# Decoder layer on one core: the FFN step in two token halves, low value weights last, and another end stage

## The chip, the cores and the metric

The kernel runs on 1 core of one Trainium2 chip. The metric is the device time of one execution in microseconds (us), lower is better. Engines: PE (TensorE matmul; PEld its weight loads), DVE (VectorE), ACT (ScalarE), POOL (GpSimd), SP (SyncE, which issues the DMAs here). They run side by side and are ordered by semaphores alone.

## The reference

One decoder layer on 512 tokens of width 1024, then a last RMSNorm, all in float32:

```
h  = RMSNorm(x) * (1+scale1) + shift1;  proj = h @ w_in
merged = sigmoid(gA) * (hgrn2(proj) @ W_a) + sigmoid(gB) * (attention(proj) @ W_b)
x  = x + (1+gate1) * (merged @ w_out)                        # w_out 1024x1024
h2 = RMSNorm(x) * (1+scale2) + shift2
u_gate, u_val = split(h2 @ w_up)                             # w_up 1024x5632
x  = x + (1+gate2) * ((gelu(causal_conv3(u_gate)) * u_val) @ w_down)
out = RMSNorm(x)
```

## The kernel before, in words

Every float32 product is made of three passes: an operand `a` is split in a high part (ACT copies it to fp32r) and a low part (`a - high`, a subtraction), and PE adds high*high, low*high and high*low in one PSUM bank. Weights come in units of 1 MB through two raw buffers, slots 0 and 1. For each unit SP issues the load (L465) once the slot's last unit is split, ACT makes the high part (L659, one instruction), POOL the low part (L590, four). Units 38 to 41 are `w_out` (the out-projection), 42 to 63 are `w_up`, in turn a gate unit and a value unit, and 64 to 74 are `w_down`.

**Out-projection.** Each of the four units makes four tiles (tokens t = 0..3, 128 tokens by 256 columns, 8 k steps of 3 matmuls). DVE multiplies a tile by the row of (1+gate1) into an SBUF buffer `sgb` (L1620) and adds it to the residual stream `x1` (L1622). ACT squares the new columns and sums them (L870). After the last unit's columns DVE adds up the four sums of a tile (L1628), POOL makes `rstd` of it in two instructions (L551, L552), and ACT or DVE scales the tile to `xn_ffn` (L878: tiles 0, 1 and half of 3; L1647: tile 2 and half of 3).

**Hand-over to the FFN step.** PE transposes the 4 x 8 blocks of `xn_ffn`, tile by tile, into 8 banks (L937). Per k block (128 features by 512 tokens) DVE makes `h_tmp2` with scale and shift (L1339), ACT makes `h_hi` (L891), and the low part `h_lo` is made on DVE (even k and k = 1, L1301) or POOL (odd k from 3, L583). On POOL these stand behind the low part of unit 43, the first value unit. Then a loop of 11 turns runs, each a gate unit and a value unit of 48 matmuls of 512 columns; the gate unit runs k outermost over two banks and in its first turn waits for `h_lo` of each k. ACT and DVE do the convolution, GELU and product with the value (L898 to L1675).

**End stage.** The down product fills the 8 banks `y(t, half)` (512 columns each). In the last unit they become ready one by one. For each, DVE multiplies by the row of (1+gate2) into `gelu` (L1685) and adds it to `x1` (L1686); ACT squares (L921); POOL multiplies tiles 0 and 1 by the final gain into `xg` (L645), and for every tile adds the two sums (L648) and makes `rstd` (L551, L552). ACT scales `xg` (L914) for tiles 0, 1 and 3; DVE makes `xg` of tile 3 (L1688) and the whole of tile 2 (L1691). SP sends each piece out (L526).

## Time and profile before

| | |
|---|---|
| median of 3 runs | 1010.56 us (1008.28 to 1012.77) |
| the profiled execution | 1011.39 us, its span 1009.7 us |
| PE busy | 954.7 us, 95% of the span, 4911 matmuls |
| DVE / ACT / POOL busy | 466.9 / 367.9 / 463.4 us |
| DMA | 111.33 MB, queue q1 33.3% |
| PE granted clock, mean | 0.982 |
| the output's DMAs, issue to landing | 2.6 us for 512 KB, 2.1 us for 256 KB (medians) |

Start times in rows are us from the span's start. A row of the timeline has the start, the duration, the engine, the line and the operation; in brackets stands how long the engine sat idle before it and what released it. A matmul's duration is longer than the distance to the next one, since they are pipelined. PEclk 1.00 is full speed.

### The profile page before, as it was taken

The page shows a single profiled execution, that of the slowest core. Times are in us where ns is not written, and L with a number is a line of the kernel's source. Part 1 is how long each engine was busy: PE and PEld are TensorE (multiplying, and loading weights), DVE is VectorE, ACT ScalarE, POOL GpSimd, SP SyncE. Part 2 cuts the span into 40 slices and gives each one's busy share as a digit, 9 for nine tenths or more (in the row PEclk, how much of TensorE's full clock was granted, in tenths as well). Part 3 has the DMA queues.
Part 4 walks back from the last instruction along what each step waited for, and adds up shares of the span by engine and source line. Part 5 has one row for each costly group of instructions (what it writes and reads, how often), then busy time and mean ns, then how long its engine had stood idle before and what let it go on. Part 6 is the DMA issues. An engine that isn't in the chain of part 4 may idle for free.

```text
span 1009.7 us, 12653 instructions
## 1 busy us (share of the span) xinstructions
PE 954.7 (95%) x4911; PEld 812.8 (80%) x4911; DVE 466.9 (46%) x720; ACT 367.9 (36%) x499; POOL 463.4 (46%) x382
## 2 busy tenths in 40 slices
PE   2699999999999989899999999899999999999995
PEld 2578989998888878788778899688888888888884
DVE  5855366665337858886642554622222322200006
ACT  6443332424234141444222334544435544412113
POOL 3669542534123243534455455553543453453544
PEclk9989999999999989999999999999999999999998
DMA  9722222121151756362222533123223223223212
GB/s 322 223 83 84 84 84 84 43 84 43 43 167 43 242 175 217 117 209 84 83 84 84 188 101 109 42 83 122 86 83 125 83 83 109 100 87 122 84 42 83
DMA packets 94817, 111.33 MB, mean 110 GB/s; under 512 B 1930, under 2 KB 88118, under 8 KB 94774
## 3 DMA queue, kind: packets, MB, share of 16 engines
q1 hardware_dynamic: 94774, 110.72, 33.3%
q8 instruction: 31, 0.51, 0.2%
q14 instruction: 12, 0.10, 0.0%
HBM read 108.62 MB, written 2.10 MB: 110 GB/s over the span
## 4 chain that ended last, share of the span: by engine, by line
PE 43%; issue 31%; POOL 18%; DVE 5%; ACT 1%; DMA 1%; SPq 0%; POOLq 0%; ACTq 0%; DVEq 0%
PE bank L934 43%; POOL w_lo L590 17%; DVE x L1686 1%; DVE part L1284 1%; DMA x_in<-in_x_dram 1%; DVE h_lo L1301 1%; DVE gelu L1685 0%; DVE part L1295 0%; DVE ada L1284 0%; DVE part L1286 0%; DVE ada L1286 0%; ACT w_hi L659 0%; DVE part L1291 0%; POOL rstd L551 0%; ACT xn_in L703 0%
## 5 line engine op out<-in xcount | busy, mean ns | idle before, releaser
L590 POOL TENSOR_TENSOR w_lo<-w_raw,w_hi 128x512 fp32r<-128x512 f32 x292 | 395.8, 1386 | 494.1 <-ACT w_hi L659 494.1
L934 PE MATMUL bank<-h_hi,w_hi 128*128 128x512 f32 x832 | 332.8, 400 | 9.1 <-POOL w_lo L590 6.0
L934 PE MATMUL bank<-h_hi,w_lo 128*128 128x512 f32 x832 | 329.1, 396 | 0.0
L934 PE MATMUL bank<-h_lo,w_hi 128*128 128x512 f32 x832 | 328.7, 395 | 0.0
L659 ACT ACTIVATE w_hi<-w_raw 128x2048 fp32r<-128x2048 f32 x73 | 139.4, 1909 | 238.1 <-PE bank L934 180.8
L934 PEld LDWEIGHTS bank<-h_hi,w_hi 128*128 128x128 f32 x832 | 159.8, 192 | 44.4 <-POOL w_lo L590 6.2
L934 PEld LDWEIGHTS bank<-h_hi,w_lo 128*128 128x128 f32 x832 | 159.0, 191 | 33.9
L934 PEld LDWEIGHTS bank<-h_lo,w_hi 128*128 128x128 f32 x832 | 159.7, 192 | 32.9
L934 PE MATMUL bank<-w_lo,act_hi 128*128 128x512 f32 x176 | 68.5, 389 | 0.0
L934 PE MATMUL bank<-w_hi,act_lo 128*128 128x512 f32 x176 | 68.5, 389 | 0.0
L934 PE MATMUL bank<-w_hi,act_hi 128*128 128x512 f32 x176 | 68.5, 389 | 0.0
L1660 DVE SCALAR_TENSOR_TENSOR conv<-bank,convc,conv 128x511 f32<-128x511 f32 x22 | 16.4, 745 | 107.8 <-ACT conv L898 107.8
L1685 DVE TENSOR_TENSOR gelu<-bank,g_row 128x512 f32<-128x512 f32 x8 | 5.5, 682 | 107.9 <-PE bank L934 107.9
L1284 DVE SCALAR_TENSOR_TENSOR part<-ada,csilu,part 128x256 f32<-128x256 f32 x64 | 43.8, 685 | 0.0
L1670 DVE TENSOR_TENSOR gelu<-gelu,bank 128x512 f32<-128x512 f32 x22 | 15.1, 687 | 58.3 <-PE bank L934 45.2
L898 ACT ACT_TABLE_LOAD x11 | 14.1, 1283 | 73.8 <-PE bank L934 73.8
L934 PEld LDWEIGHTS bank<-w_hi,act_hi 128*128 128x128 f32 x176 | 33.0, 188 | 6.9
L934 PEld LDWEIGHTS bank<-w_hi,act_lo 128*128 128x128 f32 x176 | 33.0, 188 | 6.9
L934 PEld LDWEIGHTS bank<-w_lo,act_hi 128*128 128x128 f32 x176 | 33.0, 188 | 6.7
L1284 DVE SCALAR_TENSOR_TENSOR ada<-ada,csilu 128x256 f32<-128x256 f32 x56 | 37.4, 669 | 0.0
L934 PE MATMUL bank<-w_hi,m_hi 128*128 128x256 f32 x128 | 36.3, 284 | 0.3 <-POOL w_lo L590 0.3
L934 PE MATMUL bank<-w_hi,h_hi 128*128 128x256 f32 x128 | 36.5, 285 | 0.0
(247 smaller groups left out, 1329.2 us busy)
## 6 DMA issues: line engine op xcount, KB each, us to landing
w_raw<-in_w_in_dram SPq DMA_DIRECT2D x32, 1024.0 KB, 5.2
ada<-in_w_ada_dram SPq DMA_DIRECT2D x24, 1024.0 KB, 7.2
w_raw<-in_w_up_dram SPq DMA_DIRECT2D x22, 1024.0 KB, 5.1
w_raw<-in_w_down_dram SPq DMA_DIRECT2D x11, 1024.0 KB, 4.8
w_raw<-in_w_out_dram SPq DMA_DIRECT2D x4, 1024.0 KB, 6.5
x_in<-in_x_dram SPq DMA_DIRECT2D x4, 512.0 KB, 7.1
w_raw<-in_w_in_dram SPq DMA_DIRECT2D x8, 256.0 KB, 8.5
w_raw<-in_w_branch_a_dram SPq DMA_DIRECT2D x2, 1024.0 KB, 4.9
```

Of the source, the lines that this page charges most:

```text
L590: ins = pool.tensor_tensor(wlo[slot][:, cols], raw[slot][:, cols], whi[slot][:, cols].bitcast(F32), ALU.subtract)
L659: act.activation(whi[bufs][:, :], raw[bufs][:, :], ACT.Copy).then_inc(hi_done, 1)
L898: act.activation(conv[:, t, :], bank[t][:, :], ACT.Identity, scale=CW[:, bass.ds(2 * i + (2 * FT + t), 1)], bias=CW[:, bass.ds(2 * i + (3 ...
L934: return pe.matmul(o, lhsT, rhs, start=start, stop=stop, **kw)
L1284: ins = stt(dst, unit[:, k, :], sc, dst, ALU.mult, ALU.add)
L1301: tt(h_lo[:, k, :], h_part(which, k), h_hi[:, k, :].bitcast(F32), ALU.subtract).then_inc(h_lo_done[k % 2], 1)
L1660: stt(tt_, bank[t][:, 0:S - 1], CW[:, bass.ds(2 * i + (FT + t), 1)], tt_, ALU.mult, ALU.add).then_inc(tap_done, 1)
L1670: tt(gelu[:, t, :], gelu[:, t, :], bank[bk][:, :], ALU.mult).then_inc(free[bk], 1)
L1685: link(tt(gelu[:, half, :], b[:, :], g2_row[:, cols], ALU.mult))
L1686: tt(x1[:, t, cols], x1[:, t, cols], gelu[:, half, :], ALU.add).then_inc(x2_done, 1)
```

## The change

1. Out-projection: DVE multiplies inside the PSUM bank and adds from there to `x1`; `sgb` is not used.
2. Last out-projection unit (41): the order of DVE is written out in `last_tiles`; the mean of the first three column sums is taken beforehand (`mean3`), so that POOL needs one instruction (`root2`) per tile. In PE's last tile, tokens 384 to 511, the transposes of tokens 0 to 255 stand between k = 3 and k = 4.
3. The gate unit's first turn is taken out of the loop and runs in two token halves of 256 columns, each 8 k steps of 6 matmuls. The transposes of the second half stand behind k = 5 of the first half. `h_tmp2`, `h_hi` and `h_lo` are made per half, two k blocks to a bank. Transposes use banks 4 to 7; the gates use banks 0 and 2, which the last out-projection tile (bank 1) doesn't use; the values use 1 and 3.
4. First value unit (43): the 32 matmuls with its high weights come first, then the 16 with the low ones; on ACT and POOL its split comes later than before. In all later value units k is outermost and both banks end together.
5. End stage: multiply inside the bank as in 1; POOL weighs tiles 0, 1, half of 2 and half of 3, DVE finishes the other halves in one instruction each; the last two roots are one POOL instruction each; the last four output pieces are 256 KB each.

The diff, cut to its core, in the order planner of the banks, POOL, ACT, PE, DVE:

```diff
-    for k in range(KT):
-        use(("xT", 1, k), "gates" if k < 3 else "small")
+    for half in range(2):
+        for j in range(KT // 2):
+            use(("xT2", half, j), "turn")
     base = list(uses)
-    for i, name in enumerate(("gate0", "gate1", "val0", "val1")):
+    last = table["g", U_UP - 1, 3][0]
+    for name, i in zip(("gate0", "gate1", "val0", "val1"), [b for b in range(3) if b != last] + [last, 3]):
...
+            def low_h2(half, k):
+                pool.wait_ge(h2_hi_done, half * KT + k + 1)
+                pool.tensor_tensor(h_lo[:, k, HALF[half]], h2_part(half, k), h_hi[:, k, HALF[half]].bitcast(F32),
+                                   ALU.subtract).then_inc(h2_lo_done[half][1], 1)
...
+            def root2(t):
+                pool.wait_ge(ssq_done, t + 1)
+                pool.tensor_tensor(rstd[:, TT + t:TT + t + 1], ssq[:, TT + t:TT + t + 1], mhalf[:, 0:1],
+                                   ALU.pow).then_inc(rstd_done, 1)
...
-            for t in range(TT):
-                pool.wait_ge(ssq_done, t + 1)
-                inverse_root(TT + t, 1)
-            low_part(U_UP + 1, 1)
-            pool.wait_ge(h_lo_done[1], KT // 2 + 1)
-            for k in range(3, KT, 2):
-                low_h(1, k)
+            for t in range(TT - 1):
+                root2(t)
+            low_h2(0, 1)
+            root2(TT - 1)
+            for k in range(3, KT, 2):
+                low_h2(0, k)
+            for k in range(1, KT, 2):
+                low_h2(1, k)
+            low_part(U_UP + 1, 1)
...
+            def final_weight(t, cols):
+                pool.wait_ge(x2_done, 2 * t + (2 if cols.stop == D else 1))
+                pool.tensor_tensor(xg[:, t, cols], x1[:, t, cols], gf_row[:, cols], ALU.mult).then_inc(xg_done, 1)
+            def last_root(t):
+                col = 2 * TT + t
+                pool.wait_ge(mean_last, t - (TT - 2) + 1)
+                pool.tensor_tensor(rstd[:, col:col + 1], ssq[:, col:col + 1], mhalf[:, 0:1], ALU.pow).then_inc(rstd_done, 1)
...
+            for t in range(TT - 2):
+                final_weight(t, slice(0, D))
...
                 inverse_root(col, 1)
+            final_weight(TT - 2, slice(512, D))
+            last_root(TT - 2)
+            final_weight(TT - 1, slice(0, 512))
+            last_root(TT - 1)
...
+                        if u == U_UP - 1 and t == 2:
+                            xn_again(0, slice(0, D))
+                        if u == U_UP - 1 and t == TT - 1:
+                            for k in range(2):
+                                high_h2(0, k)
...
+            def high_h2(half, k):
+                j = k // 2
+                b, n = BANKS["xT2", half, j]
+                if k % 2:
+                    evacuated(act, ("xT2", half, k // 2))
+                else:
+                    act.wait_ge(h2_tmp_done, half * KT // 2 + k // 2 + 1)
+                act.activation(h_hi[:, k, HALF[half]], h2_part(half, k), ACT.Copy).then_inc(h2_hi_done, 1)
...
+            for k in range(2, 6):
+                high_h2(0, k)
             xn_again(TT - 1, slice(512, D))
+            for k in range(6, KT):
+                high_h2(0, k)
             high_part(1, 8 * (U_UP + 2))
             for k in range(KT):
-                evacuated(act, ("xT", 1, k))
-                act.activation(h_hi[:, k, :], h_part(1, k), ACT.Copy).then_inc(h_hi_done, 1)
+                high_h2(1, k)
...
             for t in range(TT):
+                square(t, 0)
+                if t == TT - 1:
+                    act.wait_ge(rstd_done, 2 + TT + t - 1)
+                    scaled_out(t - 1, slice(512, D), y_last[1])
+                square(t, 1)
                 if 0 < t < TT - 1:
-                    act.wait_ge(xg_done, t)
+                    act.wait_ge(rstd_done, 2 + TT + t - 1)
                     scaled_out(t - 1, slice(0, D), y_done)
...
+                        if u == U_UP - 1 and t == TT - 1:
+                            token_tile(b[:, 0:256], parts, merged, plain_tokens(t), range(KT // 2))
+                            turned(0)
+                            kts = range(KT // 2, KT)
...
+            def first_values():
+                hi, lo = (w[1][:, :].rearrange("p (k c) -> p k c", c=256) for w in (whi, wlo))
+                pe.wait_ge(hi_done, U_UP + 2)
+                for bk, n in two_banks("val"):
+                    pe.wait_ge(free[bk], n)
+                for k in range(KT):
+                    for t, (bk, _) in enumerate(two_banks("val")):
+                        for a in (h_hi, h_lo):
+                            mm(bank[bk][:, :], hi[:, k, t * P:(t + 1) * P], a[:, k, :], k == 0 and a is h_hi, False,
+                               skip_group_check=True)
+                pe.wait_ge(lo_done, U_UP + 2)
+                for t, (bk, _) in enumerate(two_banks("val")):
+                    for k in range(KT):
+                        ins = mm(bank[bk][:, :], lo[:, k, t * P:(t + 1) * P], h_hi[:, k, :], False, k == KT - 1,
+                                 skip_group_check=True)
+                    ins.then_inc(full[bk], 1)
+            parts = unit_parts(U_UP, 0, 256)
...
+            for half in range(2):
+                for k in range(KT):
+                    h2_low_wait(pe, half, k)
+                    up_step(two_banks("gate"), parts, k, HALF[half], half == 1)
+                    if half == 0 and k == 5:
+                        turned(1)
+            first_values()
...
+            def residual(u, t):
+                cols = slice(256 * (u - U_OUT), 256 * (u - U_OUT) + 256)
+                b = ready(dve, ("g", u, t))
+                link(tt(b[:, 0:256], b[:, 0:256], g1_row[:, cols], ALU.mult))
+                release(tt(x1[:, t, cols], x1[:, t, cols], b[:, 0:256], ALU.add), ("g", u, t))
...
+            def last_tiles():
+                u = U_UP - 1
+                dve.wait_ge(ssp_done, 3 * TT)
+                link(dve.tensor_reduce(mean3[:, :], ssp[:, :].rearrange("p (t v) -> p t v", v=4)[:, :, 0:3], AX_X, ALU.add))
+                link(ts(mean3[:, :], mean3[:, :], 1.0 / D, EPS, ALU.mult, ALU.add))
+                residual(u, 0)
+                residual(u, 1)
+                mean_square(0)
+                mean_square(1)
+                xn_again(1, slice(0, D))
+                residual(u, 2)
+                mean_square(2)
+                for k in range(2):
+                    make_h2(0, k)
+                low_h2(0, 0)
+                residual(u, TT - 1)
+                for k in range(2, 4):
+                    make_h2(0, k)
+                mean_square(TT - 1)
+                low_h2(0, 2)
+                xn_again(2, slice(0, D))
+                for k in range(4, 6):
+                    make_h2(0, k)
+                low_h2(0, 4)
+                xn_again(TT - 1, slice(0, 512))
+                for k in range(6, KT):
+                    make_h2(0, k)
+                low_h2(0, 6)
+                for k in range(KT):
+                    make_h2(1, k)
+                    if k % 2:
+                        low_h2(1, k - 1)
...
+            def mean(t):
+                col = 2 * TT + t
+                dve.wait_ge(sq_done, TT + 2 * t + 1)
+                link(ts(ssq[:, col:col + 1], ssp[:, 2 * t:2 * t + 1], 1.0 / D, EPS, ALU.mult, ALU.add))
+                dve.wait_ge(sq_done, TT + 2 * t + 2)
+                stt(ssq[:, col:col + 1], ssp[:, 2 * t + 1:2 * t + 2], 1.0 / D, ssq[:, col:col + 1], ALU.mult,
+                    ALU.add).then_inc(mean_last, 1)
...
+            t, cols = TT - 1, slice(512, D)
+            mean(t)
             dve.wait_ge(x2_done, 2 * TT)
-            tt(xg[:, TT - 1, :], x1[:, TT - 1, :], gf_row[:, :], ALU.mult).then_inc(xg_last, 1)
-            t = TT - 2
             dve.wait_ge(rstd_done, 2 + TT + t)
-            stt(x1[:, t, :], x1[:, t, :], rstd[:, 2 * TT + t:2 * TT + t + 1], gf_row[:, :], ALU.mult,
+            stt(x1[:, t, cols], x1[:, t, cols], rstd[:, 2 * TT + t:2 * TT + t + 1], gf_row[:, cols], ALU.mult,
+                ALU.mult).then_inc(y_last[3], 1)
+            t, cols = TT - 2, slice(0, 512)
+            stt(x1[:, t, cols], x1[:, t, cols], rstd[:, 2 * TT + t:2 * TT + t + 1], gf_row[:, cols], ALU.mult,
                 ALU.mult).then_inc(y_last[0], 1)
 
 

```

DVE's instructions at the hand-over, from the third tile of unit 41. In the names `bank1` is a PSUM bank, `ssp` and `ssq` are the sums of squares, `a2` and `mod` scale and shift. Before:

```order
L1620 TENSOR_TENSOR sgb_105<-bank1,g1_row_109 128x256 [waits bank_full1]
L1622 TENSOR_TENSOR x1_108<-x1_108,sgb_105 128x256 [waits bank_free1]
L1628 TENSOR_REDUCE ssq_149<-ssp_150 128x1 [waits ssp_done] x2
L1647 TENSOR_SCALAR xn_ffn_112<-x1_108,rstd_151 128x1024 [waits rstd_done]
L1647 TENSOR_SCALAR xn_ffn_112<-x1_108,rstd_151 128x512 [waits rstd_done]
L1339 TENSOR_SCALAR h_tmp2a_113<-bank0,a2_147,mod_140 128x512 [waits bank_full0]
L1339 TENSOR_SCALAR h_tmp2a_113<-bank1,a2_147,mod_140 128x512 [waits bank_full1]
L1301 TENSOR_TENSOR h_lo_59<-h_tmp2a_113,h_hi_58 128x512 [waits h_hi_done] x2
```

Now:

```order
L1753 TENSOR_SCALAR xn_ffn_112<-x1_108,rstd_152 128x1024 [waits rstd_done]
L1743 TENSOR_TENSOR bank0<-bank0,g1_row_109 128x256 [waits bank_full0]
L1744 TENSOR_TENSOR x1_108<-x1_108,bank0 128x256 [waits dve_chain]
L1748 SCALAR_TENSOR_TENSOR ssq_149<-ssp_150,mean3_151 128x1 [waits ssp_done]
L1458 TENSOR_SCALAR h_tmp2a_113<-bank4,a2_147,mod_140 128x256 [waits bank_full4] x2
L1420 TENSOR_TENSOR h_lo_59<-h_tmp2a_113,h_hi_58 128x256 [waits h2_hi_done]
L1743 TENSOR_TENSOR bank1<-bank1,g1_row_109 128x256 [waits bank_full1]
L1744 TENSOR_TENSOR x1_108<-x1_108,bank1 128x256 [waits dve_chain]
L1458 TENSOR_SCALAR h_tmp2b_114<-bank5,a2_147,mod_140 128x256 [waits bank_full5] x2
L1748 SCALAR_TENSOR_TENSOR ssq_149<-ssp_150,mean3_151 128x1 [waits ssp_done]
L1420 TENSOR_TENSOR h_lo_59<-h_tmp2b_114,h_hi_58 128x256 [waits h2_hi_done]
```

The first two blocks of the first half now stand ahead of the residual of the last tile (`bank1`), and the scaling of tile 1 ahead of the residual of tile 2 (`bank0`).

POOL from the roots to the low part of unit 43 (`w_lo1`), before:

```order
L551 TENSOR_SCALAR rstd_151<-ssq_149 128x1 [waits ssq_done]
L552 TENSOR_TENSOR rstd_151<-rstd_151,mhalf_157 128x1 [waits pool_chain]
L590 TENSOR_TENSOR w_lo1_54<-w_raw1_50,w_hi1_52 128x512 [waits hi_done]
L590 TENSOR_TENSOR w_lo1_54<-w_raw1_50,w_hi1_52 128x512 x3
L583 TENSOR_TENSOR h_lo_59<-h_tmp2b_114,h_hi_58 128x512 [waits h_hi_done,h_lo_odd]
```

Now:

```order
L621 TENSOR_TENSOR rstd_152<-ssq_149,mhalf_158 128x1 [waits ssq_done] x3
L615 TENSOR_TENSOR h_lo_59<-h_tmp2a_113,h_hi_58 128x256 [waits h2_hi_done]
L621 TENSOR_TENSOR rstd_152<-ssq_149,mhalf_158 128x1 [waits ssq_done]
L615 TENSOR_TENSOR h_lo_59<-h_tmp2b_114,h_hi_58 128x256 [waits h2_hi_done]
...
L615 TENSOR_TENSOR h_lo_59<-h_tmp2b_114,h_hi_58 128x256 [waits h2_hi_done]
L628 TENSOR_TENSOR w_lo1_54<-w_raw1_50,w_hi1_52 128x512 [waits hi_done]
```

All eight odd blocks of both halves now stand ahead of the low weights.

ACT's last instructions, from the first squares of tile 2, before:

```order
L921 ACTIVATE squares,ssp<-x_108 128x512 [waits x2_done] x2
L914 ACTIVATE x_108<-xg,rstd 128x1024 [waits rstd_done,xg_done]
L921 ACTIVATE squares,ssp<-x_108 128x512 [waits x2_done] x2
L914 ACTIVATE x_108<-xg,rstd 128x512 [waits rstd_done,xg_last]
L914 ACTIVATE x_108<-xg,rstd 128x512 [waits rstd_done]
```

Now:

```order
L984 ACTIVATE x_108<-xg,rstd 128x1024 [waits xg_done,rstd_done]
L991 ACTIVATE squares,ssp<-x_108 128x512 [waits x2_done]
L984 ACTIVATE x_108<-xg,rstd 128x512 [waits xg_done,rstd_done]
L991 ACTIVATE squares,ssp<-x_108 128x512 [waits x2_done]
L984 ACTIVATE x_108<-xg,rstd 128x512 [waits xg_done,rstd_done]
```

The squares of tile 3's second half now stand behind the scaling of half of tile 2, which waits for POOL's third root.

## Rows read from the trace of the kernel before

**Rows 1.** Stretches: length, then busy PE, PEld, DVE, ACT, POOL, PEclk, DMA share, GB/s

```profile
482.00:484.00 2.00, 0.85 (x4) 0.38 (x2) 1.97 (x2) 1.11 (x2) 0.00 (x0) 1.00 0.77 258
486.00:488.00 2.00, 2.00 (x6) 1.54 (x6) 1.87 (x3) 0.00 (x0) 2.00 (x3) 0.50 0.00 0
628.00:630.00 2.00, 2.00 (x19) 1.88 (x19) 0.91 (x3) 1.73 (x4) 0.19 (x1) 1.00 1.06 372
634.00:636.00 2.00, 0.00 (x0) 0.00 (x0) 1.37 (x2) 1.68 (x3) 1.28 (x2) 1.00 0.00 0
636.00:638.00 2.00, 1.32 (x3) 1.16 (x4) 2.00 (x2) 0.00 (x0) 2.00 (x2) 0.52 0.00 0
```

**Rows 2.** Timeline of PE at the hand-over

```profile
628.55 1.99 PE L937 MATMUL bank<-ident,xn_ffn 128*128 128x128 f32 x16
631.46 2.30 PE L937 MATMUL bank<-ident,xn_ffn 128*128 128x128 f32 x16 [0.91 <-DVE xn_ffn L1647]
636.68 0.77 PE L934 MATMUL bank<-h_hi,w_hi 128*128 128x512 f32 x1 [2.92 <-DVE h_lo L1301]
...
649.73 0.39 PE L934 MATMUL bank<-h_lo,w_hi 128*128 128x512 f32 x1
649.96 0.39 PE L934 MATMUL bank<-h_hi,w_lo 128*128 128x512 f32 x1
```

**Rows 3.** Timeline of DVE at the hand-over

```profile
623.00 0.42 DVE L1620 TENSOR_TENSOR sgb<-bank,g_row 128x256 f32<-128x256 f32 x1 [0.88 <-PE bank L934]
623.45 1.34 DVE L1622 TENSOR_TENSOR x<-x,sgb 128x256 f32<-128x256 f32 x1
...
628.75 0.42 DVE L1620 TENSOR_TENSOR sgb<-bank,g_row 128x256 f32<-128x256 f32 x1 [1.91 <-PE bank L934]
629.21 0.42 DVE L1622 TENSOR_TENSOR x<-x,sgb 128x256 f32<-128x256 f32 x1
...
630.65 0.75 DVE L1647 TENSOR_SCALAR xn_ffn<-x,rstd 128x1024 f32<-128x1024 f32 x1 [0.28 <-POOL rstd L552]
...
633.03 1.53 DVE L1339 TENSOR_SCALAR h_tmp2a<-bank,a,mod 128x512 f32<-128x512 f32 x2 [0.43 <-PE bank L937]
```

**Rows 4.** Timeline of ACT at the hand-over

```profile
627.22 2.18 ACT L878 ACTIVATE xn_ffn<-x,rstd 128x1024 f32<-128x1024 f32 x2
629.67 0.42 ACT L870 ACTIVATE xn_ffn<-x 128x256 f32<-128x256 f32 x1 [0.27 <-DVE x L1622]
...
632.75 1.90 ACT L659 ACTIVATE w_hi<-w_raw 128x2048 fp32r<-128x2048 f32 x1
```

**Rows 5.** Timeline of POOL at the hand-over

```profile
620.54 5.41 POOL L590 TENSOR_TENSOR w_lo<-w_raw,w_hi 128x512 fp32r<-128x512 f32 x4 [6.11 <-ACT w_hi L659]
...
634.72 5.89 POOL L590 TENSOR_TENSOR w_lo<-w_raw,w_hi 128x512 fp32r<-128x512 f32 x4 [2.63 <-ACT w_hi L659]
...
643.34 1.29 POOL L583 TENSOR_TENSOR h_lo<-h_tmp2a,h_hi 128x512 fp32r<-128x512 f32 x1 [1.03 <-ACT h_hi L891]
```

**Rows 6.** Timeline of all engines, end stage

```profile
988.44 0.69 DVE L1685 TENSOR_TENSOR gelu<-bank,g_row 128x512 f32<-128x512 f32 x1 [107.87 <-PE bank L934]
...
991.33 2.40 POOL L645 TENSOR_TENSOR xg<-x,gf_row 128x1024 f32<-128x1024 f32 x1 [8.20 <-DVE x L1686]
...
991.82 2.46 DVE L1686 TENSOR_TENSOR x<-x,gelu 128x512 f32<-128x512 f32 x1
...
997.43 0.39 PE L934 MATMUL bank<-w_hi,act_lo 128*128 128x512 f32 x1
998.04 0.64 POOL L648 TENSOR_TENSOR ssq<-ssp 128x1 f32<-128x1 f32 x1
...
999.05 0.55 POOL L552 TENSOR_TENSOR rstd<-rstd,mhalf 128x1 f32<-128x1 f32 x1
...
1001.92 0.69 DVE L1686 TENSOR_TENSOR x<-x,gelu 128x512 f32<-128x512 f32 x1
...
1005.84 1.33 ACT L914 ACTIVATE x<-xg,rstd 128x512 f32<-128x512 f32 x2 [2.48 <-POOL rstd L552]
```

More of the change, by code:

```diff
@@ new lines, in up_step, with up_tiles @@
+            def up_step(bks, parts, k, cols, last):
+                for t, (bk, _) in enumerate(bks):
+                    ins = three_passes(bank[bk][:, cols], [a[:, k, t * P:(t + 1) * P] for a in parts],
+                                       [a[:, k, cols] for a in (h_hi, h_lo)], k, KT - 1, skip=True)
+                    if k == KT - 1 and last:
+                        ins.then_inc(full[bk], 1)
+            def up_tiles(name, half, i):
+                parts = unit_parts(2 * i + U_UP + half, half, 256)
+                for bk, n in two_banks(name):
+                    pe.wait_ge(free[bk], i + n)
+                for k in range(KT):
+                    up_step(two_banks(name), parts, k, slice(0, S), True)
```

220 lines of the change are left out of this document (109 added, 111 removed).

## The prediction, made blind

> **What bounds the kernel now.** First the page's busy table: PE is busy 95% of the span and its clock is 0.982 on average, so time can come only from the few places where PE stands still, runs slowly, or has already ended. Then the waits of PE by stretch and the timeline of two places. *Hand-over to the FFN step* [rows 2]: out-projection ends at 628.55; 16 transposes (1.99 us), 0.91 idle, 16 more, 2.92 idle for the first `h_lo`, and the gate unit runs from 636.68 to 649.96 + 0.23 = 650.19. From 628.55 that is 21.64 us, in which the 48 matmuls need 48 x 0.227 = 10.9. The rest, 10.7, is 4.0 of transposes, 3.8 of idle, and 2.6 lost in the unit, because the granted clock fell to 0.52 after the long idle [rows 1, 2]. *End stage* [rows 6]: PE's last matmul starts at 997.43, the last scaling ends at 1005.84 + 1.33 = 1007.17. A tile of 512 columns is ready every 6 x 0.227 = 1.36 us, and DVE needs 0.69 + 0.69, overlapping to 1.34. It would keep pace, yet an add with both inputs in SBUF takes 2.46 instead of 0.69 beside a POOL instruction that starts just before it and takes 2.40. That happens twice, 1.77 and 1.70, and the last add ends at 1002.61.
>
> **The hand-over, step by step** (times of the old trace; up to tile 1's residual nothing moves). A tile of out-projection is 2.88 us, so a 256-column matmul costs 0.12: 623.00 to 628.75 is two tiles [rows 3]. DVE starts 0.2 after a tile's end.
> - *Residual in the bank.* With one input in PSUM the add should take 0.42 beside POOL, not 1.34 [rows 3]: L1620 reads a bank and stays at 0.42 while POOL works [rows 3, 5]. Writing a product to PSUM has no row; between 0.42 as to SBUF and +0.2 each I take 0.42. Here the gain is hidden, since POOL's low part of unit 42 ends at 625.95 [rows 5] before any root.
> - *Roots.* One POOL instruction of 0.55, the 128x1 power [rows 6], instead of two: tile 0 at 626.6, tile 1 at 627.3. ACT scales tile 0 in 1.14 [rows 4] to 627.8, DVE tile 1 in 0.75 [rows 3] to 628.05.
> - *PE.* Tile 3's first 12 matmuls end at 625.67 + 1.44 = 627.1. PE waits 1.0 (less one transpose), transposes until 630.0, and ends the other 12 matmuls at 631.4.
> - *First half.* Everything on 256 columns: DVE block 0.45 to 0.5 (0.77 for 512 [rows 3], in proportion 0.38, plus a fixed part), subtraction 0.42, ACT copy 0.42 [rows 4], POOL subtraction 0.7 (1.29 for 512 [rows 5]). DVE does tile 2's residual 628.05 to 628.9; squares and root follow; blocks 0 and 1 to 630.6, the low part of block 0 to 631.1: ready when PE is (631.4). Blocks 0 and 1 take PE 1.44, to 632.9. DVE takes tile 3's residual at 631.65 to 632.5, blocks 2 and 3 to 633.4, low part of 2 to 634.0: PE waits 1.2. Then comes tile 2's scaling, 0.75, with POOL's low part behind it on the shared inputs; blocks 4 and 5 are ready at 636.2: PE waits 0.5. Blocks 4 and 5 end at 637.8, the second transposes at 639.8, blocks 6 and 7 at 641.2.
> - *Second half.* A pair of blocks costs DVE 2 x 0.48 + 0.42 = 1.4 and PE 1.44. ACT's high part of unit 43 stands ahead of it, 1.9 [rows 4], and ends at 640.0; the first low part follows at 640.9. PE needs it at 641.2, just in time, and runs through: 641.2 + 5.8 = 647.0.
> - *Sum.* 650.2 - 647.0 = **3.2 us**. The 96 half-width matmuls cost 11.5 against 10.9, which is in it.
> - *First values.* Unit 43's low part now starts after the last `h_lo`, about 645.7, and takes 5.4 to 5.9 [rows 5]: 651.6. PE reaches its low weights after 32 x 0.227 = 7.3, at 654.2. Cost nothing, cover 2.6. Behind it on POOL stands unit 44 (its high part is ready about 651), done by 657.0; PE needs it at 657.9. This is the thinnest cover, 0.9; SP's load of unit 45 waits for the same low part and lands about 5 us later, early enough. In later turns both value banks end together; DVE and ACT finish about 1 us after them as the second bank does now, nothing.
>
> **The end stage** (old times, so that only its own gain counts). Without the two blocked adds, each x1 piece is 1.42 behind its bank: 988.44 + 7 x 1.36 + 1.42 + 0.4 for the tiny mean instructions = 999.8 for the last, 2.8 earlier. That isn't all paid out, because POOL is now the chain: `xg` of tile 0 from 991.3, 2.4 + 1.56 (998.04 to 999.60 is sum and root [rows 6]), tile 1 the same to 999.2, half of tile 2 (1.25) and root to 1001.2. ACT scales the half of tile 2 to 1001.95, and only then squares tile 3's second half, 0.81 with the read of the sum, 1002.75. Mean on DVE and root on POOL: 1003.45. DVE's two halves of 0.69 end at 1004.8. Old 1007.17, so **2.4 us**. Both unknowns are small: if POOL's half `xg` costs the full 2.4, the gain is 0.1; if the root of tile 2 never blocks ACT, it is 3.2.
>
> **Sum.** -3.2 - 2.4 = -5.6 us. The profiled execution had 1011.39, so 1005.8; it lies 0.8 above the median of the runs, 1010.56, which gives **1005.0 us**. What a measurement of this kernel can tell from no change is about 0.5%, 5.05 us, so the forecast is just past that edge.
>
> **A rule that speaks against it.** The rows: PE did transposes alone from 628.55 with 0.91 idle between, and PEclk stayed 1.00 in the slices at 628 and at 634; it was 0.52 only after the idle of 2.92 [rows 1, 2]. In the new order no single idle is over 1.3. The Trainium skill (TensorE: Matmul & The Clock Gate, Part 4: PE-mode transpose) says that transposes don't count as activity in the way matmuls do. By that rule the stretch from 627.1 to 630.0 would be one idle of 2.9 us and the clock would fall in it, as in the first rival; by the rows, it stays up. The trace doesn't bear the rule out, though it shows no long stretch of transposes alone.
>
> **Rivals.**
> - *The clock falls once* (0.17). For: several short idles lie within 10 us, and around 483 an idle with PE busy only 0.85 of 2.00 us was enough to have 0.50 at 486 [rows 1]. Against: the slices above. Price: the old fall cost 2.6 less 0.2 of idle; part of it is swallowed by idle that exists anyway. 1.4 to 2.4, so 1006.4 to 1007.4.
> - *DVE becomes the bound of the new stage* (0.13). It has 8 more instructions per half than before and three roots, each a round trip over ACT and POOL, in front of PE's first half. If each of some 30 steps is 0.1 longer than I took, the gates end at 650: only the end pays, 1008.2. Against: the widths are from rows.
> - *The end pays nothing* (0.07): ACT, waiting for POOL's root before the last squares, ends near 1007: 1007.3.
> - *Slower* (0.05): the clock stays at half for the whole of the first half and into the second, since PE now never has a long run of matmuls there. From 627.8 to 647.0 PE has 12 + 96 matmuls (13.0) and 32 transposes (4.0); at half speed that is 17 more less 2.7 of idle, up to +14; if it lasts to the second half only, +8.5. Less 5.6: from +2.9 to +8.7, 1013.5 to 1019. It decides if the low clock lasts past about 639.
> - *It doesn't do what it says* (0.03): the first values wait after all, because POOL is late for unit 43 or 44 by over 0.9 us: each us late is one us lost, about 1007.
>
> **How the numbers follow.** The forecast has 0.55, with its own range 1003.2 to 1006.8; about 0.8 of it lies below 1005.5. Faster by over 0.5%: 0.55 x 0.8 + a little of the first rival = 0.47. Slower by over 0.5%: 0.04. Within: 0.49. The range takes in the forecast, the fall of the clock and the DVE rival: 1002.8 to 1008.6.
>
> **What would show it.** Right: PE's transposes in two groups near 628 and 638, no idle over 1.3 us, PEclk 1.00 throughout, gate unit ending at 647, values at 658 without a wait on `w_lo`; in the end stage no DVE add over 0.75 us, and about 7.4 us from the last matmul's start to the last scaling, where there were 9.7. Wrong: PEclk under 0.9 in any slice between 627 and 642; a wait for `h_lo` in the second half; adds from PSUM that still stretch beside POOL; or a wait for `w_lo` in unit 43 or 44.

## The result and the profile after

The changed kernel took **1002.03 us** (median of 7 runs, 996.26 to 1004.9). Seven runs of the kernel before gave 1010.56 (1006.61 to 1013.98). The ratio is 0.9918 with a 95% interval of 0.9891 to 0.9945. The forecast was 1005.0, with a range from 1002.8: the median lies 3.0 below the forecast and 0.8 below the range.

The page of the changed kernel:

```profile
span 994.3 us, 12780 instructions
PE 948.6 (95%) x4959; PEld 810.6 (82%) x4959; DVE 454.1 (46%) x738; ACT 368.8 (37%) x506; POOL 460.2 (46%) x381
PEclk9999999999999999999999999999999999999998
PE 43%; issue 30%; POOL 20%; DVE 4%; ACT 1%; DMA 1%; POOLq 0%; SPq 0%; DVEq 0%; ACTq 0%
```

The span is 15.4 shorter than in the trace before (1009.7). To see where that lies, each trace is cut at marks that both kernels have. **A** runs from the start to DVE's multiply of the second tile of unit 41, 623.00 before [rows 3] and 613.98 now. Ahead of it the change touches only the residuals of the out-projection's units 38 to 41, which are now in the bank (point 1), and PE doesn't wait for those: from ACT's high part of unit 26 to the mark the two traces take 200.84 and 200.80 us. **B** runs from there to the first multiply of the end stage, 988.44 before [rows 6] and 975.89 now. **C** runs to the end of the last scaling, 1007.17 before and 990.51 + 0.75 = 991.26 now. The tail is what is left of the span.

| us | A | B | C | tail |
|---|---|---|---|---|
| before | 623.00 | 365.44 | 18.73 | 2.53 |
| after | 613.98 | 361.91 | 15.37 | 3.04 |
| difference | -9.02 | -3.52 | -3.36 | +0.51 |

So B, C and the tail, where the change acts, give **-6.4 us** against the -5.6 of the prediction. The other 9.0 lie in A, ahead of the out-projection, in code that is the same in both. Whether A's part belongs to the change at all is the first question for the experiments.

PE at the new hand-over, timeline:

```profile
618.45 1.94 PE L1013 MATMUL bank<-ident,xn_ffn 128*128 128x128 f32 x16 [0.19 <-ACT xn_ffn L932]
620.14 0.36 PE L1010 MATMUL bank<-w_hi,m_hi 128*128 128x256 f32 x1
...
624.15 0.39 PE L1010 MATMUL bank<-h_hi,w_hi 128*128 128x256 f32 x1 [0.90 <-DVE h_lo L1420]
...
625.40 0.39 PE L1010 MATMUL bank<-h_hi,w_hi 128*128 128x256 f32 x1 [0.28 <-POOL h_lo L615]
...
647.83 0.39 PE L1010 MATMUL bank<-h_hi,w_hi 128*128 128x512 f32 x1
```

Where [rows 2] had idles of 0.91 and 2.92, there are now 0.19, 0.90 and 0.28, and none in the second half. The last row is the second gate unit's first matmul: the first value unit starts 48 x 0.227 = 10.9 before it, at 636.92, which is the end of the first gate unit. The clock, by stretch (columns as in [rows 1]):

```profile
622.00:624.00 2.00, 1.25 (x11) 1.05 (x9) 1.97 (x6) 1.19 (x4) 0.33 (x2) 1.00 0.00 0
624.00:626.00 2.00, 1.57 (x11) 1.37 (x12) 1.97 (x5) 0.81 (x3) 1.35 (x2) 1.00 0.00 0
628.00:630.00 2.00, 2.00 (x21) 2.00 (x20) 0.99 (x2) 2.00 (x3) 0.69 (x1) 1.00 0.00 0
```

It stayed at 1.00 (2.4 GHz), where the old stage had 0.52 at 636 [rows 1]. DVE, ACT and POOL there:

```profile
614.78 1.81 DVE L1748 SCALAR_TENSOR_TENSOR ssq<-ssp,mean 128x1 f32<-128x1 f32 x2
617.67 0.75 DVE L1753 TENSOR_SCALAR xn_ffn<-x,rstd 128x1024 f32<-128x1024 f32 x1 [1.07 <-POOL rstd L621]
618.34 0.42 DVE L1743 TENSOR_TENSOR bank<-bank,g_row 128x256 f32<-128x256 f32 x1
618.79 0.42 DVE L1744 TENSOR_TENSOR x<-x,bank 128x256 f32<-128x256 f32 x1
```

```profile
617.14 1.16 ACT L932 ACTIVATE xn_ffn<-x,rstd 128x1024 f32<-128x1024 f32 x1 [1.74 <-POOL rstd L621]
...
627.78 1.90 ACT L711 ACTIVATE w_hi<-w_raw 128x2048 fp32r<-128x2048 f32 x1
```

```profile
611.53 5.05 POOL L628 TENSOR_TENSOR w_lo<-w_raw,w_hi 128x512 fp32r<-128x512 f32 x4 [6.47 <-ACT w_hi L711]
616.54 1.09 POOL L621 TENSOR_TENSOR rstd<-ssq,mhalf 128x1 f32<-128x1 f32 x2
...
635.30 5.05 POOL L628 TENSOR_TENSOR w_lo<-w_raw,w_hi 128x512 fp32r<-128x512 f32 x4
641.57 5.04 POOL L628 TENSOR_TENSOR w_lo<-w_raw,w_hi 128x512 fp32r<-128x512 f32 x4 [1.21 <-ACT w_hi L711]
```

Two things to read here. POOL's low part of unit 42 takes 5.05 where it took 5.41 [rows 5], since no add with two SBUF inputs stands in its way, and the roots follow 0.36 sooner. And the covers of the prediction hold: unit 43's low weights are ready at 640.35 and needed at 636.92 + 7.3 = 644.2, unit 44's at 646.61 and 647.83, so 3.9 and 1.2 are left (forecast 2.6 and 0.9).

The end stage, DVE and then POOL; the last two DVE rows are the last scalings:

```profile
978.56 0.69 DVE L1846 TENSOR_TENSOR bank<-bank,g_row 128x512 f32<-128x512 f32 x1
979.28 0.69 DVE L1847 TENSOR_TENSOR x<-x,bank 128x512 f32<-128x512 f32 x1
...
986.27 0.69 DVE L1847 TENSOR_TENSOR x<-x,bank 128x512 f32<-128x512 f32 x1
...
989.85 0.75 DVE L1855 SCALAR_TENSOR_TENSOR x<-x,rstd,gf_row 128x512 f32<-128x512 f32 x1 [0.75 <-POOL rstd L690]
990.51 0.75 DVE L1858 SCALAR_TENSOR_TENSOR x<-x,rstd,gf_row 128x512 f32<-128x512 f32 x1
```

```profile
978.79 2.42 POOL L684 TENSOR_TENSOR xg<-x,gf_row 128x1024 f32<-128x1024 f32 x1 [8.21 <-DVE x L1847]
981.16 0.20 POOL L696 TENSOR_TENSOR ssq<-ssp 128x1 f32<-128x1 f32 x1
981.45 0.19 POOL L577 TENSOR_SCALAR rstd<-ssq 128x1 f32<-128x1 f32 x1
981.72 0.55 POOL L578 TENSOR_TENSOR rstd<-rstd,mhalf 128x1 f32<-128x1 f32 x1
982.25 2.41 POOL L684 TENSOR_TENSOR xg<-x,gf_row 128x1024 f32<-128x1024 f32 x1
```

The add that took 2.46 beside POOL [rows 6] takes 0.69 beside the same POOL instruction (979.28 lies within 978.79 + 2.42). POOL's sum of two numbers takes 0.20 where it took 0.64 [rows 6].

### The profile page after: what moved, and what is told of

It reads as the page before. It is cut to its first block, busy times and chain, and to the rows that moved or that the text cites. A ratio compares the mean times of both kernels' runs of the same rounds, so it can differ in the third digit from the quotient of the medians.

```text
span 994.3 us, 12780 instructions
## 1 busy us (share of the span) xinstructions
PE 948.6 (95%) x4959; PEld 810.6 (82%) x4959; DVE 454.1 (46%) x738; ACT 368.8 (37%) x506; POOL 460.2 (46%) x381
## 4 chain that ended last, share of the span: by engine, by line
PE 43%; issue 30%; POOL 20%; DVE 4%; ACT 1%; DMA 1%; POOLq 0%; SPq 0%; DVEq 0%; ACTq 0%
PE bank L1010 43%; POOL w_lo L628 18%; DMA x_in<-in_x_dram 1%; DVE part L1398 1%; POOL xg L684 1%; DVE part L1409 0%; DVE ada L1398 0%; DVE part L1400 0%; DVE ada L1400 0%; ACT w_hi L711 0%; PE bank L1013 0%; DVE part L1405 0%; DVE h_lo L1415 0%; ACT xn_in L755 0%; POOL rstd L578 0%
## 5 line engine op out<-in xcount | busy, mean ns | idle before, releaser
L1010 PE MATMUL bank<-h_hi,w_hi 128*128 128x512 f32 (+1 forms) x848 | 332.8, 393 | 3.6 <-POOL w_lo L628 2.4
L1010 PE MATMUL bank<-h_lo,w_hi 128*128 128x512 f32 (+1 forms) x848 | 329.2, 388 | 0.0
L1010 PE MATMUL bank<-h_hi,w_lo 128*128 128x512 f32 (+1 forms) x848 | 326.5, 388 | 0.0
L1846 DVE TENSOR_TENSOR bank<-bank,g_row 128x512 f32<-128x512 f32 x8 | 5.6, 696 | 107.9 <-PE bank L1010 107.9
L1398 DVE SCALAR_TENSOR_TENSOR part<-ada,csilu,part 128x256 f32<-128x256 f32 x64 | 40.8, 637 | 0.0
L1010 PE MATMUL bank<-w_lo,h_hi 128*128 128x256 f32 x128 | 36.2, 283 | 0.0
```

Of the source, the lines that this page charges most:

```text
L1010: return pe.matmul(o, lhsT, rhs, start=start, stop=stop, **kw)
L1398: ins = stt(dst, unit[:, k, :], sc, dst, ALU.mult, ALU.add)
L1846: link(tt(b[:, :], b[:, :], g2_row[:, cols], ALU.mult))
```

## The experiments

Each number below is from one trace of that kernel. A, B, C and the tail are cut as above; `u20-26` is the time between ACT's high parts of units 20 and 26, a piece of A.

| kernel | A | u20-26 | B | C | tail |
|---|---|---|---|---|---|
| before | 623.00 | 86.49 | 365.44 | 18.73 | 2.53 |
| before_again | 614.98 | 78.31 | 365.43 | 18.73 | 2.46 |
| after | 613.98 | 78.79 | 361.91 | 15.37 | 3.04 |
| after_again | 625.45 | 86.58 | 361.93 | 15.37 | 3.05 |
| new_end | 623.28 | 85.59 | 365.47 | 15.37 | 2.98 |
| old_end | 615.18 | 78.82 | 361.92 | 18.73 | 2.47 |
| add_end | 621.03 | 83.50 | 361.92 | 19.27 | 2.98 |
| add_out | 620.68 | 83.21 | 362.40 | 15.36 | 3.06 |
| val3 | 617.53 | 81.46 | 367.07 | 15.36 | 3.04 |
| full | 618.53 | 82.30 | 366.51 | 15.37 | 3.09 |
| end2 | 624.74 | 86.42 | 361.92 | 15.10 | 3.04 |
| better | 617.21 | 81.76 | 361.05 | 15.11 | 3.03 |
| bank_only_end | 622.34 | 83.81 | 361.91 | 15.68 | 2.47 |
| unit_first | 616.05 | 82.92 | 361.91 | 15.36 | 2.98 |
| unit_first2 | 611.67 | 82.89 | 361.93 | 15.36 | 3.04 |
| ub | 611.79 | 82.92 | 365.43 | 18.74 | 2.54 |
| best | 612.97 | 84.12 | 361.06 | 15.10 | 2.97 |

### Both kernels again: is A part of the change?

No edit. The kernel before, expected:

> The kernel before, unchanged. Three stretches of the trace: A from the start to the multiply of tile 1 in the last out-projection unit (623.00 us before, 613.98 with the change), B from there to the first multiply of the end stage (365.44 and 361.91), C from there to the end of the last scaling (18.73 and 15.37). Theory 1, the change acts only where it was made: B and C repeat to 0.2 us, ratio 1.00, and A comes out anywhere between about 612 and 625, since the same code gave both numbers. Theory 2, the changed program has a shorter A of its own: A is within 2 us of 623 here.

The kernel after, expected:

> The changed kernel, unchanged. Theory 1: B 361.9 and C 15.4 again, A scatters as in the kernel before, ratio to it 0.991 to 0.995 (6.4 us of stretches B, C and the last transfer are 0.9937). Theory 2: A within 2 us of 614 again, ratio 0.989 or lower with more rounds.

Measured: 1009.04 (12 runs) for the kernel before, ratio to itself 1.001 [0.9989, 1.0031], and 998.8 (7 runs) for the kernel after, ratio 0.9908 [0.988, 0.9936], just below the 0.991 to 0.995 expected. A is the reverse of the first pair: 614.98 for the kernel before and 625.45 for the kernel after. B and C repeat to 0.02. So the 9.0 us of A in the first pair were a matter of the single execution. They sit in units 20 to 26, in waits of PE for the low weights (POOL, `w_lo`). The waits of PE from 300 to 450, before and then before_again:

```profile
PE bank L934 <- POOL w_lo L590: 6.0, 3, 3.1
```

```profile
PE bank L934 <- POOL w_lo L590: 2.0, 2, 1.8
```

The stretch 360 to 365 in the same two:

```profile
360.00:365.00 5.00, 3.98 (x9) 3.14 (x10) 4.93 (x11) 4.84 (x17) 4.12 (x4) 0.50 0.05 17
```

```profile
360.00:365.00 5.00, 5.00 (x23) 4.08 (x23) 4.93 (x9) 3.69 (x17) 4.32 (x4) 1.00 0.01 4
```

After the idle of 3.1 the clock is 0.50 (1.2 GHz) for some us, after the one of 1.8 it stays up; in the four longest traces (`u20-26` over 85) this happens twice there. The trace of after has 2.4 us of these waits, the longest 2.2, and no fall in these units; after_again has 5.8, the longest 3.2, and the fall.

### The two halves of the change apart

**new_end** is the kernel before with the end functions of the kernel after (point 5 of the change); **old_end** is the kernel after with the old ones.

```diff
-                    link(tt(gelu[:, half, :], b[:, :], g2_row[:, cols], ALU.mult))
-                    tt(x1[:, t, cols], x1[:, t, cols], gelu[:, half, :], ALU.add).then_inc(x2_done, 1)
+                    link(tt(b[:, :], b[:, :], g2_row[:, cols], ALU.mult))
+                    tt(x1[:, t, cols], x1[:, t, cols], b[:, :], ALU.add).then_inc(x2_done, 1)
...
```

> Only the end stage of the change, with all of the rest as before. Theory 1: B as before, 365.4; C 15.4 (3.4 shorter), of which about 0.5 goes back in the last transfer; ratio 0.997. Theory 2, the end's gain hangs on the order of the hand-over: C over 17. If the gain in A belongs to in-bank adds of the out-projection, A is not shorter here.

> The change without its end stage: out-projection in the bank, hand-over in halves, low value weights last. Theory 1: B 361.9 (3.5 shorter), C 18.7 as before; ratio 0.9965. Theory 2: ratio 0.992 or lower, because A is shorter by several us wherever the new hand-over code is in the program.

Measured: new_end 1004.53, ratio 0.9953 [0.9928, 0.9979]; old_end 1004.75, 0.9966 [0.9945, 0.9988]. The first lies below the 0.997 expected, which its interval still holds. In the trace new_end has C at 15.37 and B at the old 365.47; old_end has B at 361.92 and C at the old 18.73. The halves add up exactly. Less the tail (+0.5), the end is worth 2.85 (0.9972) and the hand-over 3.5 (0.9965). Both intervals hold these. All four traces with the old hand-over (ub below is the fourth) show its fall of the clock (in the two slices of 5 us there before_again has 0.84 and 0.82, from 625 to 635, and new_end 0.77 and 0.88, from 635 to 645). No trace with the new one as it stands does.

### The product in the bank, at either place

**add_end** puts the end stage's product back in SBUF and keeps all else:

```diff
-                    link(tt(b[:, :], b[:, :], g2_row[:, cols], ALU.mult))
-                    tt(x1[:, t, cols], x1[:, t, cols], b[:, :], ALU.add).then_inc(x2_done, 1)
+                    link(tt(gelu[:, half, :], b[:, :], g2_row[:, cols], ALU.mult))
+                    tt(x1[:, t, cols], x1[:, t, cols], gelu[:, half, :], ALU.add).then_inc(x2_done, 1)
```

> The change, with the product of the end stage written to SBUF again, so that its adds have both inputs there. If the blocked adds are what cost the old end stage its time: at least two adds take 2.4 us again and stretch C is 17.0 to 18.5 instead of 15.37. If POOL's chain sets the end alone, C stays within 0.4 of 15.4 although adds are blocked. B 361.9 either way.

Measured: 1006.99 in one run; C 19.27, so 3.9 more than with the product in the bank, 0.5 more than the old end stage, and above the 17.0 to 18.5 expected. Its DVE timeline:

```profile
986.34 2.46 DVE L1847 TENSOR_TENSOR x<-x,gelu 128x512 f32<-128x512 f32 x1
...
990.75 2.40 DVE L1847 TENSOR_TENSOR x<-x,gelu 128x512 f32<-128x512 f32 x1
...
995.11 1.26 DVE L1847 TENSOR_TENSOR x<-x,gelu 128x512 f32<-128x512 f32 x1
...
997.26 1.77 DVE L1847 TENSOR_TENSOR x<-x,gelu 128x512 f32<-128x512 f32 x1
```

Four adds are held up instead of two: POOL's halves for tiles 2 and 3 hold up two more. These rows agree with a rule of the Trainium skill (SBUF — State Buffer, "Who interferes with whom"): DVE and GpSimd share a port pair as an exclusive lock, and a DVE operation takes part with two SBUF inputs. With one input in PSUM it is free of it.

**bank_only_end** is the reverse: old_end with the two lines of the product alone in the bank, everything else of the end stage as before.

> The change with the old end stage, in which only the product now stays in the bank. With the product in SBUF the new order of the end gave C 19.27, the old order 18.73. If the whole gain of the end stage is the unblocked adds: DVE's last add ends 2.8 earlier than in the old one, its long scalings of tiles 3 and 2 and POOL's roots of tile 3 still get in each other's way, and C is 15.0 to 16.0, as good as the new end (15.37) within 0.6, with the old tail of 2.5. If the new distribution of work pays by itself: C over 16.5.

Measured: 1004.17 in one run; C 15.68, tail 2.47. Together 18.15, where the whole new end stage has 15.37 + 3.04 = 18.41. So the two lines carry all of the end's gain. The new distribution of work and pieces adds none: it takes 0.3 off C and puts 0.6 on the tail. Its last rows:

```profile
995.13 1.22 DVE L1821 TENSOR_TENSOR xg<-x,gf_row 128x1024 f32<-128x1024 f32 x1
...
996.62 0.99 POOL L687 TENSOR_TENSOR ssq<-ssp 128x1 f32<-128x1 f32 x1 [1.47 <-ACT squares L978]
997.69 0.19 POOL L576 TENSOR_SCALAR rstd<-ssq 128x1 f32<-128x1 f32 x1
997.96 0.55 POOL L577 TENSOR_TENSOR rstd<-rstd,mhalf 128x1 f32<-128x1 f32 x1
998.60 1.33 ACT L971 ACTIVATE x<-xg,rstd 128x512 f32<-128x512 f32 x2 [2.07 <-POOL rstd L577]
```

**add_out** puts the product of the out-projection back in an SBUF tile:

```diff
-                link(tt(b[:, 0:256], b[:, 0:256], g1_row[:, cols], ALU.mult))
+                tmp = sgb[:, t, 0:256]
+                link(tt(tmp, b[:, 0:256], g1_row[:, cols], ALU.mult))
...
```

> The change, with the out-projection's product in SBUF again. If my missing 0.5 us at the roots comes from POOL's low part of unit 42 being free of DVE's adds (5.05 us with the change, 5.41 before): the low part takes 5.4 again, the roots come 0.4 to 0.6 later, and B is 362.4 to 362.9 instead of 361.9. If the roots don't matter: B 361.9.

Measured: 1003.44 in one run; B 362.40, 0.5 more, and POOL's low part of unit 42 takes 5.41 again. PE waits 0.7 for `xn_ffn` where it waited 0.2: the root comes that much later behind POOL's low part. The prediction had this gain as hidden; it is worth 0.5.

### The low value weights last, and the halves

**val3** gives the first value unit the order of the other units, three products per k:

```diff
-            first_values()
+            up_tiles("val", 1, 0)
```

> The change, but the first value unit does its three passes per k as the later ones do, so PE needs the low weights at once. If they are hidden only by coming last: PE waits for w_lo from the end of the gate unit to the end of POOL's low part, 3.4 us by the changed kernel's trace (636.92 to 640.35), B 365.3. If the low part would have been ready anyway: B 361.9. The clock may fall in a wait of 3.4 us, then up to 2 us more.

Measured: 1004.97 in one run; B 367.07, 5.2 more, at the upper end of what was expected. PE waits 3.25 for the low weights, and from 645 to 650, right behind that wait, the clock is 0.71:

```profile
643.90 0.50 PE L1010 MATMUL bank<-h_hi,w_hi 128*128 128x512 f32 x1 [3.25 <-POOL w_lo L628]
```

```profile
645.00:650.00 5.00, 5.00 (x18) 3.93 (x17) 0.81 (x2) 2.49 (x4) 4.87 (x4) 0.71 0.65 210
```

Without this part the hand-over would be slower than before (B was 365.44).

**full** takes the halves away: all transposes first, then both halves of each k:

```diff
-            for half in range(2):
-                for k in range(KT):
+            turned(1)
+            for k in range(KT):
+                for half in range(2):
...
```

> The change, with PE's part of the halves taken out: all transposes of the second half first, then the gate unit over 512 columns, each k when both its halves are split; DVE, ACT and POOL keep their order. If the halves are what hides the second half's work: PE can do k = 0 only at about 631 in the times of the changed kernel, after 9 us with only 16 transposes in it, so B is 4 to 6 us longer (366 to 368), and the clock falls again. If the gain is only the earlier transposes and roots: B within 1 us of 361.9.

Measured: 1005.17 in one run; B 366.51, 4.6 more. Waits of PE from 615 to 660:

```profile
PE bank L1013 <- DVE xn_ffn L1752: 3.1, 1, 3.1
PE bank L1013 <- ACT xn_ffn L932: 1.8, 2, 1.6
PE bank L1010 <- DVE h_lo L1419: 0.4, 1, 0.4
```

The idle moves back ahead of the transposes. The idle is followed by a clock of 0.66 from 630 to 635. What the halves do is fill it with the 36 gate matmuls of k = 0 to 5 that need only tokens 0 to 255.

### Better orders

**end2** changes the order at the very end: ACT squares tile 3's second half before it scales tile 2, and DVE scales its half of tile 2 before the last mean.

```diff
+                square(t, 1)
                 if t == TT - 1:
...
-                square(t, 1)
```

> The change, with two moves in the end stage: ACT squares the last half of tile 3 before it scales half of tile 2, and DVE finishes its half of tile 2 before the mean of tile 3 instead of last. By the rows of the changed kernel the square ends 0.5 earlier, POOL's last root is bound by its own weights (done 0.5 before the root now) and comes 0.4 earlier, and one scaling of 0.66 leaves the end: C 14.2 to 14.4 instead of 15.37. If POOL's chain is all that counts: 14.7 to 14.9.

Measured: 1006.49 in one run, C 15.10: 0.3 gained, of the 1.0 or so expected. The scaling that I moved forward has two SBUF inputs and met POOL's half `xg`:

```profile
998.20 1.27 POOL L684 TENSOR_TENSOR xg<-x,gf_row 128x512 f32<-128x512 f32 x1
998.26 1.75 DVE L1853 SCALAR_TENSOR_TENSOR x<-x,rstd,gf_row 128x512 f32<-128x512 f32 x1 [0.53 <-POOL rstd L690]
```

It took 1.75 instead of 0.75, and the last mean stood behind it.

**better** is end2 and, at the hand-over, blocks 2 and 3 of the first half before tile 3's residual (on DVE, ACT and POOL), since PE's longest idle (0.90) was for block 2's low part. Blocks 4 and 5 also come ahead of tile 2's scaling, and ACT's high part of unit 43 comes later.

```diff
+                for k in range(2, 4):
+                    make_h2(0, k)
+                low_h2(0, 2)
                 residual(u, TT - 1)
-                for k in range(2, 4):
-                    make_h2(0, k)
...
```

> The end of end2, and at the hand-over blocks 2 and 3 of the first half, and the low part of 2, ahead of tile 3's residual, blocks 4 and 5 ahead of tile 2's scaling, and ACT's high part of unit 43 behind block 3 of the second half. PE's waits of 1.06 and 0.43 at k = 2 and 4 should become 0 and about 0.5, and B 360.5 to 361.2 instead of 361.9. If DVE's total work sets the pace whatever its order: B 361.9. With the end, 1.5 to 2.3 us less than the change; ratio to the kernel before about 0.990 to 0.993, which this measurement cannot tell from the change's own.

Measured: 999.85 (6 runs), ratio 0.993 [0.9908, 0.9952]; B 361.05, 0.87 less, as expected.

### The load order in stretch A

SP issues the load of unit u + 1 behind two loads of `w_ada` in the units where two are due, and the second of these waits for DVE's partial sums. SP's waits from 300 to 450, before:

```profile
SPq L506 <- DVE part L1291: 130.6, 14, 17.6
```

In that part of a long trace PE waits for low weights, so this delay is the suspect. Unit 21 shows it: its load was issued at 344.01 and landed at 353.93 in the trace of before, and at 343.07 and 352.62 in before_again. What makes it later in one execution than in another isn't shown: SP's waits are nearly the same in both (125.1 us in before_again). If it is the cause, a load issued ahead of the second `w_ada` load must end the waits, in either kernel. **unit_first** (and **unit_first2**, the same again beside the next two), **ub** (the same edit to the kernel before) and **best** (to better):

```diff
-                if u >= 3:
+                if u >= 3 and len(MOD_UNITS.get(u - 1, ())) < 2:
...
-                for n in MOD_UNITS.get(u, ()):
+                for i, n in enumerate(MOD_UNITS.get(u, ())):
+                    if i == 1 and u + 1 < U_OUT:
+                        load_unit(u + 1, unit_source(u + 1), (u + 1) % 2)
```

> The change, with the load of the next weight unit issued ahead of the second of two w_ada loads in the units that have two. In the units 20 to 26 PE waits 2.0 to 2.4 us for w_lo in the short traces (stretch of 78.3 to 78.8 us) and 5.8 to 6.0 in the long ones (85.6 to 86.6), with the clock at half speed after each wait of 3. If SP's queue, where the unit's load stands behind a w_ada load that waits for DVE, makes the unit late: the waits go and the stretch is under 78 us. If the w_ada sums get later in turn, DVE holds the banks longer and the stretch is 80 or more, with waits on DVE.

> unit_first again, for a second trace. From unit 3 to the hand-over mark it took 543.7 us, where the twelve traces of kernels with the old order of loads have 543.6 to 553.7. If the order of loads removes the long waits: 543 to 546 again, no wait for w_lo over 1 us between 300 and 450, clock 1.00 there. If one trace was luck: 547 or more, with such a wait.

> The kernel before, with the load order of unit_first alone. If the scatter belongs to the weight loads and not to the change: from unit 3 to the mark 543 to 546 here too, B 365.4 and C 18.7 as before, ratio to the kernel before 0.995 to 0.998. If the load order only worked beside the change: 547 to 554.

> The kernel of better, with the weight loads of unit_first. B 361.05 and C 15.1 as measured apart; the stretch from unit 3 to unit 26 is 340.7 as in the one trace of unit_first, so A about 614 to 617. Median 995 to 999, ratio 0.985 to 0.991 if the unit loads take away the scatter of A; 0.993 as in better if they don't.

Measured: unit_first 997.78, ratio 0.9899 [0.9834, 0.9963]; unit_first2 995.64, 0.9874 [0.9841, 0.9908]; ub 1001.75, 0.9937 [0.9914, 0.996]; best **993.87** (992.58 to 995.82), 0.985 [0.9821, 0.988], the fastest kernel here. In the one trace of each, PE's wait for `w_lo` between 300 and 450 is gone (in ub the load of unit 21 is issued at 339.48 and has landed at 347.21). This is all that PE waits for there in ub and in best:

```profile
PE bank L936 <- DVE part L1293: 0.8, 1, 0.8
```

```profile
PE bank L1014 <- DVE part L1409: 1.9, 2, 1.1
```

The clock at 360 to 370 and at 405 to 410 is 1.00 in each. Their A is 611.67 to 616.05, where it ran from 613.98 to 625.45 in the rest. The start of the program scatters too, by 2.8 us up to unit 3; counted from unit 3's high part A is 540.5 to 543.7 in these four and 543.6 to 553.7 in the others.

Not all came as expected. `u20-26` was to be under 78 in unit_first and is 82.9. By the words of that expectation this is the rival, which also has the wait on DVE (0.8). But the load order moves ACT's high parts themselves, and from unit 3 to unit 26 the four take 340.7 (341.9 in best), less than any trace with the old order (342.7 to 350.9). From unit 3 to the mark, unit_first2 (542.1) and ub (540.5) lie below the 543 to 546 expected, and so do the ratio of ub (0.995 to 0.998 expected) and the median of best (995 to 999).

So the long waits hang on the load order and not on the change: the same edit takes them out of the kernel before. best is 0.015 below the kernel before where after is 0.008. It isn't shown that all of the scatter goes. There is one trace of each kernel, and the runs of ub still lie from 1000.18 to 1005.99. A part of it is elsewhere, between unit 26 and the mark, which takes 199.8 to 203.0. There every trace has an idle of PE of 1.57 to 1.59 us for `wg_lo`, between 471 and 485. Behind it the clock is at 0.50 for 3.4 us in some traces and 6.8 us in others, and in ub it doesn't fall.

## Why the prediction was off, step by step

**The size of the change: right within 0.8 us.** -5.6 was forecast, -6.4 is what B, C and the tail show, the same in every pair. The mechanisms were the ones named. Their sizes:

- *Hand-over, -3.2 forecast, -3.5 measured, from two errors that nearly cancel.* I read the old gate unit's end as 650.19 from [rows 2], but the listing stopped at 650, and 48 matmuls counted from 636.68 end before the row at 649.50 (51 rows start between 636.6 and 650, and the last three are the value unit's). So the old end was 0.7 too late, the fall of the clock cost 1.9 in the unit and not 2.6, and -2.5 would have been the honest sum. The new stage in turn ended at 636.92 + 9.02 = 645.94 in old times, 1.06 ahead of the 647.0 worked out. The row behind the 48 matmuls, in the trace of before:

```profile
649.50 0.39 PE L934 MATMUL bank<-h_hi,w_hi 128*128 128x512 f32 x1
```

- *Where the new stage was faster.* PE's wait before the transposes was 0.19, not 1.0: the roots came some 0.5 earlier, mostly because POOL's low part of unit 42 shrank from 5.41 to 5.05 (the residual in the bank, which I had costed at nothing; add_out gives 0.5 for it), and 16 transposes between matmuls hold PE for 620.14 - 618.45 = 1.7, not 2.0. The waits at k = 2 and 4 were 0.90 and 0.28 as idle, and 1.06 and 0.43 counted from start to start, against 1.2 and 0.5. The widths on 256 columns were right: 0.43 and 0.42 for the residual in the bank, 0.99 for two blocks, 0.73 on POOL.
- *First values: right.* No wait on low weights, covers 3.9 and 1.2.
- *End, -2.4 forecast, -3.36 in C and +0.5 in the tail.* The mis-sized term is POOL's chain: I took 1.56 for a sum and a root from a row that was held up itself (0.64 + 0.55 and more [rows 6]); with no DVE instruction on the lock it is 982.25 - 981.16 = 1.1. It is on the chain twice, 0.9 in all, which is nearly the 0.96 that C fell short of the forecast; the smaller differences of the other terms about cancel. From PE's last matmul start (984.88) to the last scaling's end it took 6.4; forecast 7.4, old 9.7. The tail was not in the sum, +0.5. SP issues the last three pieces within 0.85 us (990.51, 990.88, 991.36), and they take 2.02, 2.35 and 2.53 us to land; the old last two took 2.03 and 2.08. That they hold each other up is likely and not tested.

**The number: wrong by 3.0, because of the base of the sum.** The step that failed is the one from -5.6 to 1005.0: it put the sum on one trace with an A of 623.0 and on the median of three runs, 1010.56, with nothing said of their scatter. The 8 us that units 20 to 26 of A take more in a long trace than in a short one are more than the whole effect, and neither the sum nor the range had a term for them, though the runs of before stood 4.5 us apart. 0.8 of the miss is the local sum (6.4 against 5.6). The other 2.2 are scatter of A as far as the runs tell: the first 48 runs of the kernel before have a mean of 1008.4, 2.1 below the base, and 1008.4 - 6.35 is 1002.05, where the changed kernel measured 1002.03. That it agrees so well is luck, since the seven runs of before that stand beside it, the forecast's three among them, also have a median of 1010.56. In 7 runs of after the mean clock went from 0.985 to 0.992 and the time from 1004.9 to 996.26, and the clock and the time go together, as the falls in A would make them; only one of the seven has a trace. The ratio that B, C and the tail give is 0.9937 (6.35 of 1008.4). It lies within the first interval (0.9891 to 0.9945) and 0.0001 above the second (0.988 to 0.9936). Whether the change itself makes the short A somewhat likelier is not settled: 14 runs of after have a mean of 1001.0, 7.4 below the 48, and with some 3 us of scatter a run the mean of 14 is uncertain by about 0.9 (an estimate), as much as the 1.0 in question.

**The rivals.** The clock never fell in the new stage (1.00 in every window of 610 to 637, in after, after_again and old_end), so neither the first rival nor the slower one came about. DVE was not the bound: PE waited 1.2 us for `h_lo` in all, in the first half only. The end did pay. The values didn't wait. The fall after the idle of 1.57 at 483, from which the first rival was argued, comes in 16 of the 17 traces, so the worry had a ground; at the new hand-over no trace shows one. *The rule that spoke against it* isn't borne out: the Trainium skill (TensorE: Matmul & The Clock Gate, Part 4) says that transposes don't count as activity in the way matmuls do; here 0.19 idle and 1.7 of transposes, and later another 16 after two idles, left the clock at 1.00. At the hand-over it fell only in kernels that idle 2.9 us or more there.

**The chances.** Faster by over 0.5% had 0.47, and it is what the measurement shows: the interval's upper end, 0.9945, is below 0.995. The forecast's own range, 1003.2 to 1006.8, had 0.55 and missed by 1.2, and so did the whole range, by 0.8. No rival described what happened.

## What to carry to other kernels

Where DVE adds beside POOL leave one operand in PSUM: two lines that multiply inside the bank gave the whole gain of the end stage (3.0 us), and the reordering around them nothing. Where the start of a phase hangs on a chain of small operations, a half of the tokens is enough to keep PE running, but only together with what is late next (here the low weights of the next unit: without their move the stage was slower than before). Before a forecast, lay the several runs of the kernel before side by side: a spread of 4.5 us in three runs (7.4 in seven) says that something in it falls now one way and now the other, it belongs in the range, and it may be worth more than the change (the load order alone gave some 6 us).
